# The first two output blocks of three stages multiplied part by part beside the last attention, and x loaded head by head

## The reference

```
def diff_finish(o, g, subln, lam_init, w_out):
    y = rms_norm(o, subln, SUBLN_EPS) * (1.0 - lam_init)
    return (y.reshape(B, T, DA_VW) * jax.nn.silu(g)) @ w_out
...
x = x + gate * y            # end of the first block
...
y = jnp.concatenate([oa * silu(a_g), ob * silu(b_g), om * silu(m_g)], axis=-1)
return x + jnp.einsum('bte,ed->btd', y, w_out)   # end of a hybrid layer
```

## Time and profile before

| | us |
|---|---|
| median of 3 runs (2652.29 to 2657.11) | 2654.37 |
| the profiled execution, its own time | 2653.53 |
| its span | 2651.7 |
| TensorE busy | 2239.0 (84%) |
| VectorE, ScalarE, GpSimd busy | 1372.8, 1160.5, 667.8 |
| mean granted TensorE clock | 0.927 |

### The profile page before, as it was taken

One profiled execution on the slowest core, in us unless ns is written; L12 is line 12 of the kernel. 1 busy time (PEld: TensorE's weight loads), 2 busy tenths in 40 slices (PEclk: granted clock), 3 DMA queues, 4 the chain that ended last, 5 costly groups with the idle time before them and its releaser, 6 DMA issues.

```text
span 2651.7 us, 59035 instructions
## 1 busy us (share of the span) xinstructions
PE 2239.0 (84%) x25736; PEld 1640.2 (62%) x25736; DVE 1372.8 (52%) x2342; ACT 1160.5 (44%) x1933; POOL 667.8 (25%) x410
## 2 busy tenths in 40 slices
PE   8799998389888878876898888977899888898988
PEld 2577776167667767664765665654666555665656
DVE  1358788244344544444266565562455653455552
ACT  2466676143333433332254444442354453444452
POOL 0334444200011010113232222213423332433332
PEclk9899999599988999997999999987999998999998
DMA  7115454642431222222221111102111111111111
GB/s 267 57 61 174 131 162 120 181 122 75 121 94 49 65 72 61 61 68 100 84 86 36 36 33 39 34 22 86 59 55 56 56 56 57 63 56 56 48 64 64
DMA packets 148481, 211.32 MB, mean 80 GB/s; under 512 B 81920, under 2 KB 106752, under 8 KB 147456
## 3 DMA queue, kind: packets, MB, share of 16 engines
q1 hardware_dynamic: 137120, 164.28, 19.5%
q0 software_dynamic: 9952, 40.11, 5.0%
q10 hardware_dynamic: 1152, 3.15, 0.3%
HBM read 165.30 MB, written 42.21 MB: 78 GB/s over the span
## 4 chain that ended last, share of the span: by engine, by line
PE 59%; DVE 19%; ACT 10%; issue 7%; POOL 3%; DMA 2%; SPq 0%; ACTq 0%; DVEq 0%; POOLq 0%
PE ps L258 7%; PE ps L260 7%; PE ps L259 7%; PE ps L1332 3%; PE ps L538 2%; PE ps L311 2%; PE ps L1322 2%; PE ps L1347 2%; PE ps L2706 2%; PE ps L2233 2%; PE ps L391 2%; PE ps L2729 1%; PE ps L2715 1%; DVE st L2292 1%; DVE p L2306 1%
## 5 line engine op out<-in xcount | busy, mean ns | idle before, releaser
L243 POOL TENSOR_TENSOR wbl<-wb,wbh 128x1024 fp32r<-128x1024 f32 x128 | 306.3, 2394 | 603.0 <-ACT wbh L238 597.8
L258 PE MATMUL ps<-hT2h,wbh 128*128 128x512 f32 x416 | 189.9, 456 | 23.9 <-POOL wbl L243 16.5
L258 PE MATMUL ps<-hTh,wah 128*128 128x512 f32 (+1 forms) x512 | 180.6, 353 | 17.3 <-POOL wal L243 10.9
L258 PE MATMUL ps<-hT1h,wbh 128*128 128x512 f32 (+1 forms) x432 | 178.8, 414 | 3.1 <-POOL hT1l L2372 3.1
L259 PE MATMUL ps<-hTl,wah 128*128 128x512 f32 (+1 forms) x512 | 174.8, 341 | 0.0
L260 PE MATMUL ps<-hTh,wal 128*128 128x512 f32 (+1 forms) x512 | 174.7, 341 | 0.0
L260 PE MATMUL ps<-hT2h,wbl 128*128 128x512 f32 x416 | 169.5, 408 | 0.0
L259 PE MATMUL ps<-hT2l,wbh 128*128 128x512 f32 x416 | 169.4, 407 | 0.0
L238 ACT ACTIVATE wbh<-wb 128x1024 fp32r<-128x1024 f32 x128 | 134.6, 1052 | 68.8 <-PE ps L1928 43.5
L339 POOL TENSOR_TENSOR ro<-ro 128x256 f32<-128x256 f32 (+1 forms) x12 | 11.9, 993 | 580.6 <-DVE ro L323 580.6
L243 POOL TENSOR_TENSOR wal<-wa,wah 128x1024 fp32r<-128x1024 f32 x34 | 102.3, 3011 | 219.3 <-ACT wah L238 219.3
(11 more groups left out here) (400 smaller groups left out, 5704.9 us busy)
## 6 DMA issues: line engine op xcount, KB each, us to landing
wb<-in_w_in SPq DMA_DIRECT2D x56, 512.0 KB, 3.4
s_str_dram<-s POOLq DMA_DIRECT2D x48, 576.0 KB, 8.7
wm<-in_ada SPq DMA_DIRECT2D x48, 512.0 KB, 4.5
bkv<-s_str_dram SPq DMA_DIRECT2D x96, 192.0 KB, 3.4
wa<-in_rw_in SPq DMA_DIRECT2D x34, 512.0 KB, 4.2
wb<-in_da_in SPq DMA_DIRECT2D x32, 512.0 KB, 3.4
ARI<-s_str_dram SPq DMA_DIRECT2D x96, 128.0 KB, 3.5
wb<-in_w_out SPq DMA_DIRECT2D x16, 512.0 KB, 3.5
```

The lines of the kernel that those rows point to most:

```text
L243: e.tensor_tensor(self.lo[:, n % 2], self.raw[:, n % 3], self.hi[:, n % 2].bitcast(F32), ALU.subtract).then_inc(self.K.s.w_lo, 1)
L258: e.matmul(z, wh[:, k, :], hi[:, k, a:b], start=k == 0, stop=False)
```

## The change

`products_pe` yields after each k. `outputs` makes such a generator for the first two output blocks of a stage, in banks 0 and 1, each part k waiting for the low half of head k. TensorE takes one part after each of the yields 2 to 8 of the last attention (before the first it waits until banks 0 and 1 are free); the eighth part is taken in `pe_out`, which then goes on with block 2. The split of the second block's weights moves from `act_out` and `pool_out` to yield 1 of the last attention. In the output stage the sums of memory squares move from behind blocks 0, 1, 2 to behind blocks 2, 3, 4, with the sums of x 0 and 1 behind block 2. The norm's tail starts at k = 4 in place of 3, with three steps per k on ScalarE and VectorE and two on GpSimd; on ScalarE it stands behind the wait for the evacuation and the square of x. In D, SyncE loads x in eight copies, copy k when the low half of head k is signalled; weight block 43 is loaded between the seventh and the eighth.

```diff
 def products_pe(K, e, W, x, parts, ready):
...
             if k == 7:
                 m.then_inc(K.s.prod, 1)
+        yield
...
+    def outputs(self, e, l):
+
+        y, lo0, ev = self.from_y(l)
+        return products_pe(self.K, e, self.W, y, [(80 + 40 * l + k, 0, 512, k) for k in range(2)],
+                           lambda q: e.wait_ge(self.K.s.yt_lo, lo0 + q + 1))
+
+    def pe_ahead(self, e, l):
+
+        use = self.diff.use if l < 0 else self.use
+        n = len(use) if l < 0 or l == 1 else self.use0[8]
+        self.first = self.outputs(e, l)
+
+        def ahead(i):
+            if i == 2:
+                for z in range(n - 3, n):
+                    if z % 3 < 2:
+                        e.wait_ge(*use[z])
+            if 2 <= i < 9:
+                next(self.first)
+        return ahead
+
     def pe_out(self, e, l):
...
-        e.wait_ge(s.tok_c, self.c0["tok_c"] + 8 * l + 8)
-        for k in range(8):
...
+        run(self.first)
+        for k in range(2, 8):
+            run(product_pe(K, e, self.W, 80 + 40 * l + k, y, [(0, 512)], [k % 2],
+                           lambda j: e.wait_ge(s.evac_v, ev + k - 1)))
+            if l < 1:
+                for m in range(3 * k - 6, min(3 * k - 3, 8)):
                     self.nm[l + 1].pe_sum(e, m)
-            if l < 1 and k:
-                self.nx[l + 1].pe_sum(e, k - 1)
+                for m in range(k - 1 if k > 2 else 0, k):
+                    self.nx[l + 1].pe_sum(e, m)
...
+    def act_ahead(self, e, l, i):
+        if i == 1:
+            self.W.split_hi(e, 81 + 40 * l)
+
+    def pool_ahead(self, e, l, i):
+        if i == 1:
+            self.W.split_lo(e, 81 + 40 * l)
 
     def act_out(self, e, l):
...
         for k in range(8):
-            self.W.split_hi(e, 81 + 40 * l + k)
+            if k:
+                self.W.split_hi(e, 81 + 40 * l + k)
+            elif l < 1:
+                e.wait_ge(s.mem_in, 16 * l + 32)
+                for m in range(3):
+                    nm.act_square(e, m)
             if l < 1:
-                if k == 0:
-                    e.wait_ge(s.mem_in, 16 * l + 32)
-                if k < 3:
-                    for m in range(3 * k, min(3 * k + 3, 8)):
-                        nm.act_square(e, m)
-                else:
-                    run(some(tail, 2))
                 e.wait_ge(s.evac_v, ev + k + 1)
                 nx.act_square(e, k)
+                if k in (2, 3):
+                    for m in range(3 * k - 3, min(3 * k, 8)):
+                        nm.act_square(e, m)
+                elif k > 3:
+                    run(some(tail, 3))
...
     def dve_out(self, e, l):
...
         if l < 0:
-            e.wait_ge(s.x1_in, 16)
+            e.wait_ge(s.x1_in, 16 * 7)
         for k in range(8):
+            if l < 0 and k == 7:
+                e.wait_ge(s.x1_last, 16)
...
-            if k >= 3:
-                run(some(tail, 2))
+            if k >= 4:
+                run(some(tail, 3))
...
     def pool_out(self, e, l):
         tail = self.nm[l + 1].pool_tail(e) if l < 1 else iter(())
-        for k in range(8):
+        for k in range(1, 8):
             self.W.split_lo(e, 81 + 40 * l + k)
-            if k >= 3:
-                run(some(tail, 1))
+            if k >= 4:
+                run(some(tail, 2))
...
     def sp(self, e):
...
-        e.wait_ge(s.yt_lo, self.diff.c0["yt_lo"] + 8)
-        e.dma_start(self.x2[:, :, :], K.T["x1"][:, :, 256:768]).then_inc(s.x1_in, 16)
+        for k in range(8):
+            e.wait_ge(s.yt_lo, self.diff.c0["yt_lo"] + k + 1)
+            e.dma_start(self.x2[:, k, :], K.T["x1"][:, k, 256:768]).then_inc(s.x1_in if k < 7 else s.x1_last, 16)
+            if k == 6:
+                self.W.load(e, 43)
+
         e.dma_start(self.bc[:, :], K.T["bc"]).then_inc(s.tables, 16)
-        for n in range(43, 128):
+        for n in range(44, 128):
```

More of the change, by code:

```diff
@@ L119 @@
     "nr_sq nr_mul nr_rot nr_sin nr_cos nr_sum tok_t tok_c "
-    "sc_mm sm_max sm_neg sm_exp sm_df tr_mm tr_a tr_v pv_mm pv_c pv_sq pv_n at_y yt_hi yt_lo x1_in mem_in out"
+    "sc_mm sm_max sm_neg sm_exp sm_df tr_mm tr_a tr_v pv_mm pv_c pv_sq pv_n at_y yt_hi yt_lo x1_in x1_last mem_in out"
 ).split()
@@ L633, in pe_first @@
     def pe_first(self, e):
-        products_pe(self.K, e, self.W, self.hT, [(n, a, b, 2 * n + j) for n in range(2) for j, (a, b) in
-                                                 enumerate(self.cols)], lambda k: self.norm.wait_lo(e, k))
+        run(products_pe(self.K, e, self.W, self.hT, [(n, a, b, 2 * n + j) for n in range(2) for j, (a, b) in
+                                                     enumerate(self.cols)], lambda k: self.norm.wait_lo(e, k)))
     def act_mix(self, e, n, m, mucol, dst, gp=None, bonus=0):
@@ L2012, in pe_project @@
         else:
-            products_pe(K, e, self.W, self.hT, [(n, 256, 768, i % 3), (n + 1, 0, 256, (i + 1) % 3)],
-                        lambda k: self.norm.wait_lo(e, k))
+            run(products_pe(K, e, self.W, self.hT, [(n, 256, 768, i % 3), (n + 1, 0, 256, (i + 1) % 3)],
+                            lambda k: self.norm.wait_lo(e, k)))
             pk = product_pe(K, e, self.W, n + 1, self.hT, [(256, 768)], [(i + 3) % 3], lambda j: self.take(e, i + 3))
@@ L2373, in pool_split, with together @@
                         ALU.subtract).then_inc(s.yt_lo, 1)
-    def together(self, project, attend, end, split):
+    def together(self, project, attend, end, split, ahead):
         run(project(0))
@@ L2384, in together @@
                 split(h - 1)
+            ahead(h)
             h += 1
@@ L2396, in sp, with pe, act @@
             self.W.load(e, n)
-    def pe(self, e):
+    def pe(self, e, ahead):
         K, s = self.K, self.K.s
         self.together(lambda h: self.pe_project(e, h), lambda h: self.pe_attend(e, h), lambda h: self.pe_end(e, h),
-                      lambda h: None)
-    def act(self, e):
+                      lambda h: None, ahead.pe_ahead(e, -1))
+    def act(self, e, ahead):
         K, s = self.K, self.K.s
@@ L2408, in act @@
         self.together(lambda h: self.act_project(e, h), lambda h: self.act_attend(e, h), lambda h: self.act_end(e, h),
-                      lambda h: self.act_split(e, h))
+                      lambda h: self.act_split(e, h), lambda i: ahead.act_ahead(e, -1, i))
     def dve(self, e):
@@ L2526, in pe_project @@
                 self.take(e, i + j)
-            products_pe(K, e, self.W, self.hT, [(n + j, 0, 512, (i + j) % 3) for j in range(2)],
-                        lambda k: nx.wait_lo(e, k))
+            run(products_pe(K, e, self.W, self.hT, [(n + j, 0, 512, (i + j) % 3) for j in range(2)],
+                            lambda k: nx.wait_lo(e, k)))
             pk = iter(())
@@ L2813, in pool_attend, with together @@
                         ALU.subtract).then_inc(s.yt_lo, 1)
-    def together(self, l, project, attend):
+    def together(self, l, project, attend, ahead):
         run(project(8 * l))
@@ L2819, in together @@
             pace((attend(P), 10), (project(P + 1), 8))
-        run(attend(8 * l + 7))
+        for i, _ in enumerate(attend(8 * l + 7)):
+            ahead(i)
     def from_y(self, l):
@@ L2833, in pe_out @@
         y, lo0, ev = self.from_y(l)
-        e.wait_ge(s.tok_c, self.c0["tok_c"] + 8 * l + 8)
-        for k in range(8):
-            def free(j):
-                if k >= 2:
-                    e.wait_ge(s.evac_v, ev + k - 1)
-            ready = (lambda q: e.wait_ge(s.yt_lo, lo0 + q + 1)) if k == 0 else None
-            run(product_pe(K, e, self.W, 80 + 40 * l + k, y, [(0, 512)], [k % 2], free, ready))
-            if l < 1 and k < 3:
-                for m in range(3 * k, min(3 * k + 3, 8)):
+        run(self.first)
[4 more added lines that the diff above has]
+                for m in range(3 * k - 6, min(3 * k - 3, 8)):
                     self.nm[l + 1].pe_sum(e, m)
-            if l < 1 and k:
-                self.nx[l + 1].pe_sum(e, k - 1)
+                for m in range(k - 1 if k > 2 else 0, k):
+                    self.nx[l + 1].pe_sum(e, m)
         if l < 1:
             self.nx[l + 1].pe_sum(e, 7)
+    def act_ahead(self, e, l, i):
[4 more added lines that the diff above has]
+            self.W.split_lo(e, 81 + 40 * l)
     def act_out(self, e, l):
@@ L2942, in dve @@
             self.normed(e, l)
[L2943 removed]
+            self.together(l, lambda P: self.dve_project(e, P), lambda P: self.dve_attend(e, P),
+                          lambda i: None)
             self.dve_out(e, l)
@@ L3005, in _ @@
             mid.pool(e)
-            diff.pool(e)
+            diff.pool(e, second)
             second.pool(e)
@@ L3014, in _ @@
             mid.act(e)
-            diff.act(e)
+            diff.act(e, second)
             second.act(e)
@@ L3032, in _ @@
             mid.pe(e)
-            diff.pe(e)
+            diff.pe(e, second)
             second.pe(e)
```

18 lines of the change are left out of this document (10 added, 8 removed).

## The result

The changed kernel took 2681.52 us (median of 4 runs, 2679.38 to 2696.28), the kernel before 2653.33 beside it (4 runs, 2648.57 to 2657.11): ratio 1.0117, 95% interval [1.0083, 1.0152]. It is slower, by 28 us in the medians and by 22 to 40 in the interval. The profiled execution took 2679.65 us (span 2677.8, granted clock 0.925).

A forecast was written before the change was run, and what follows sets the result against it. TensorE idles in the attentions at its lower clock, a link in a chain of short steps, ahead of outputs that are TensorE alone. D +7.9, E +14.4 and F +5.4 sum to +27.7 us: 2682 us, range 2666 to 2694.

The forecast's parts named there:

- D: The first block's last attention, then its outputs; forecast to grow by 7.9 us in all.
- Attention of E and F: Last attention of the second block's layers 0 and 1: first part waits for the weight split; growth 7.4 us each.
- Attention of D: First block's last attention: VectorE held up by GpSimd's split, part 1 waits for a low half; growth 4.3 us.
- The price for no lock at all: First block's last attention: if VectorE and GpSimd shared no exclusive lock, 1.5 us cheaper, sum 26.2 in place of 27.7.
- To block 2: Start of outputs' block 2: 3.0 us earlier in D, 3.5 later in E, 7.2 after the values in F.
- Block 7: Last output block of D and E: a 4.1 us hole from the late weight split, then a 1.7 us clock fall.
- the stretch behind block 2: Outputs of D and E up to the next layer: clock fall 1.7, moved sums 3.4, Block 7 5.8 us.
- (a): All three attentions: parts keep the upper clock and fit idle time, growth -4, -5.2, -5.2; 2640 us; chance 7%.
- (b): Last output block: no hole, GpSimd's low part 5 in time; +16.1 us, 2670 us; chance 10%.
- (e): Whole change: moved blocks come off the path nowhere or are paid back exactly; 2654 us; chance 4%.
- (c): The three attentions: half of the growth is hidden, 9.6 us less; 2672 us; chance 9%.
- (d): Attentions: the lower clock level stays throughout, +11 us in E and in F, +3 in D; 2707 us; chance 8%.

The follow-up runs named there:

- Run 4: Kernel before, with only the second output block's weight split at yield 1 and TensorE's wait for it at yield 2, no product moved; 2655.06 us.
- run 9: run 8 plus, in E and F, seven three-matmul parts of block 0 at yields 2 to 8, second block's split at yield 9; 2644.66 us, ratio 0.9967.
- run 3: Changed kernel with x loaded in one copy, as before, in place of eight; 2681.03 us.
- run 5: Kernel before, with only x loaded head by head and weight block 43 loaded ahead of the last head; 2651.99 us.
- run 6: Changed kernel with ScalarE's split of weight block 82 (42 in D) ahead of the wait for mem and its squares; 2672.91 us.
- run 1: Changed kernel with GpSimd taking one low part of the mem norm at k = 5 in place of two; 2676.49 us, ratio 1.0083.
- run 2: Changed kernel with the second output block's weights split before the last attention instead of at yield 1; 2679.38 us, ratio 1.0084.
- run 7: Changed kernel with the edits of run 1, run 2 and run 6 together; 2654.35 us, the kernel before 2654.82 beside it.
- run 8: run 5 plus, in D, block 1's parts behind the attention, split at yield 9; mem's sums and norm tail one block later; 2647.29 us, ratio 0.9988.

## Why the prediction was right, and where it was off

Attention of E and F: right in its steps. The wait ahead of the first part was 3.01 (2.9), that part 2.8 (2.6), from its start to the values 15.8 (15.85), the values 1.94 (1.95); the growth 6.8 and 6.9 (7.4), as the part began 0.3 us earlier than I had it. Run 4 shows the wait as a cause by itself. What the prediction did not say is that the rest of the growth is not proportional to the size of a part: I charged each as if all of it lay on the path, which for six matmuls it nearly does and for three it does not (run 9).

Attention of D: +3.5 for 4.3, VectorE held up by the split as foreseen (2.71 us); the last transposes went 5.8 us late for 6.5. Parts 1 and 3 waited for low halves, 2.43 and 4.16. The price for no lock at all (1.5 less) is not excluded by the total alone, but by the row of L346. The row of 0.94 us that the prediction set against the lock isn't the same case: that scale reads one operand from SBUF, L346 reads two.

To block 2: D -3.56 (-3.0), E +2.7 (+3.5), F 7.4 us after the values (7.2). Runs 3 and 5 show the copy of x as what set it in D, run 6 the chain through mem in E.

Block 7: hole 4.29 and 4.24 (4.1), by the order of waits on ScalarE and GpSimd that the prediction named; gone with it in run 1.

The term that was mis-sized is the stretch behind block 2: +13.2 us in D and +13.6 in E, where 1.7 + 3.4 + 5.8 = 10.9 were forecast. Its terms for a restart at the lower level and for the hole at block 7 were too small. The prediction gave a restart eight or nine slow matmuls, 1.7 us. In the changed kernel matmuls followed each other at the slow pace (0.43 us apart in place of 0.23) for 10 and 11 of them in block 2 (D, E) and for 12 and 13 in block 7. Block 2 took 7.65 and 7.88 us where it had taken 5.61 and 5.89, so 2.0 more. From the sum ahead of block 7 to the end of that block it took 7.1 (D) and 7.2 us (E) more than before, where hole and fall were put at 5.8: TensorE idles 4.29 and 4.24 us, the block no longer starts beside the sum, and it takes 8.13 and 8.27 us for 5.88. And there was a small hole that I had not seen: 0.48 and 0.43 ahead of block 6, where GpSimd takes two steps as well, which cost 0.7 us. In E the next layer then waited 6.85 us for VectorE where it had waited 6.50. These add up to the 2.3 and 2.7 us that were missing. F lost 0.5 less than forecast.

Rivals: (a) no for the change as it stands, yes in E and F for half of it (run 9); (b) and (e) refuted; (c), half of the growth hidden, is excluded by the 6.8; (d), the lower level throughout, by the clock of 0.82 and the values.

Open: why the stretches between the stages were 0.8 us longer each in the profile after (other kernels, with nothing changed there, show 303.9 to 305.9, so that it may be scatter), and what moves D's beginning by up to 20 us from run to run. Neither was tried.

## What to carry to other kernels

Work put into an engine's idle time costs nothing only as long as it ends before the next link of the chain comes up in the same queue: size the pieces to the single gap, not to the sum of the gaps, and let none wait for something that is made at that moment. Here six matmuls a gap cost about 4 us per attention beside 2.8 for the wait; three cost none, because the values then took 1.66 us less. When steps are repacked into fewer and larger ones, look at what stands behind each on its own queue: a low half of 0.8 us, taken one block early, cost 7 us in two places.

## What the runs showed of the hardware

A hole can cost TensorE more than its length: behind the holes of 2.46 to 7.68 us ahead of blocks 2 and 7 the block took 1.6 to 2.4 us longer (7 to 13 matmuls at the slow pace), and taking away a hole of 4.3 us saved 7.1. A two-input instruction of VectorE of 0.69 us (runs 2, 7 and 8) took 2.71 beside a split on GpSimd, in every kernel that splits at yield 1. In run 9 the moved matmuls raised the granted clock of the attentions of E and F from 0.59 to 0.84 and shortened the values from 3.60 to 1.94 us, so that 21 more matmuls left the length of the attention as it was.
